# Half a weight chunk of step 28 loaded through GpSimd's queue, in seven DMAs of 17 partitions

## The reference

```
x = x + concat(retention, moba) @ w_out
h2 = rms_norm(x, norm2_w)
top_logit, top_e = top_k(h2 @ w_router + b_router, 4);  gate = softmax(top_logit)
for e in range(32):                     # for the tokens that picked e
    u = h2[tok] @ w1[e] + b1[e]         # 1024 x 2048: 8 MB of weights
    y = clamped_swiglu(u) @ w2[e] + b2[e]   # 1024 x 1024: 4 MB of weights
    x[tok] += gate * y
out = rms_norm(x, final_norm_w)
```

## Time and profile before

| | us |
|---|---|
| median of 3 runs | 1051.99 (1051.84 to 1052.05) |
| the profiled execution | 1051.63 |
| its span, first to last instruction | 1049.9 |
| outside the span | 1.7 |

### The profile page before, as it was taken

One profiled execution on the slowest core, in us unless ns is written; L12 is line 12 of the kernel. 1 busy time (PEld: TensorE's weight loads), 2 busy tenths in 40 slices (PEclk: granted clock), 3 DMA queues, 4 the chain that ended last, 5 costly groups with the idle time before them and its releaser, 6 DMA issues.

```text
span 1049.9 us, 11246 instructions
## 1 busy us (share of the span) xinstructions
PE 1029.5 (98%) x4918; PEld 415.3 (40%) x4918; DVE 221.3 (21%) x585; ACT 117.6 (11%) x223; POOL 0.2 (0%) x4
## 2 busy tenths in 40 slices
PE   9999999999999999999999999999999999999996
PEld 8888543333333333333333333333333333323332
DVE  2173442111111111111111111111111111111111
ACT  2131130000000000000000000000000000000002
POOL 0000000000000000000000000000000000000000
PEclk9999999999999999999999999999999999999999
DMA  9982999999999999999999999999999999999995
GB/s 320 369 365 81 354 364 400 410 428 424 429 428 431 433 432 428 431 429 430 432 423 431 429 435 428 434 424 433 428 428 427 430 432 431 432 429 424 428 422 214
DMA packets 39126, 424.62 MB, mean 404 GB/s; under 512 B 3512, under 2 KB 16320, under 8 KB 19744
## 3 DMA queue, kind: packets, MB, share of 16 engines
q1 hardware_dynamic: 38768, 423.51, 96.4%
q10 hardware_dynamic: 304, 0.33, 0.1%
HBM read 422.78 MB, written 1.05 MB: 404 GB/s over the span
## 4 chain that ended last, share of the span: by engine, by line
PE 89%; DMA 9%; DVE 1%; another core or an unknown queue 1%; issue 0%; ACT 0%; SPq 0%; DVEq 0%; ACTq 0%
PE PS L1444 39%; PE PS L1466 19%; DMA ring<-in_w 8%; PE PS L1122 8%; PE PS L1415 5%; PE PS L1398 4%; PE PS L1303 3%; PE PS L1259 3%; PE PS L1497 2%; PE PS L1407 2%; PE PS L1390 1%; DMA ring<-in_w_in 1%; PE PS L1571 0%; PE PS L1585 0%; PE PS L1192 0%
## 5 line engine op out<-in xcount | busy, mean ns | idle before, releaser
L1444 PE MATMUL PS<-ring,work 128*64 128x512 f32 x2040 | 450.2, 598 | 7.9 <-DMA ring<-in_w 6.8
L1444 PEld LDWEIGHTS PS<-ring,work 128*64 128x64 f32 x2040 | 143.7, 137 | 289.4 <-issue 275.8
L1466 PE MATMUL PS<-ring,work 128*64 128x512 f32 x1024 | 227.5, 596 | 0.7 <-DMA ring<-in_w 0.6
L1466 PEld LDWEIGHTS PS<-ring,work 128*64 128x64 f32 x1024 | 70.5, 137 | 154.7 <-issue 150.7
L1015 DVE TENSOR_SCALAR work<-PS 128x512 f32<-128x512 f32 x32 | 22.1, 691 | 398.3 <-PE PS L1444 398.3
L1122 PE MATMUL PS<-ring 128*128 128x256 f32 x384 | 85.4, 380 | 0.3 <-DMA ring<-in_w_in 0.3
L644 ACT ACTIVATE work<-work 128x512 f32<-128x512 f32 x32 | 20.2, 630 | 532.6 <-DVE work L1015 532.6
L1122 PEld LDWEIGHTS PS<-ring 128*128 128x128 f32 x384 | 72.0, 190 | 10.8 <-DMA ring<-in_w_in 0.7
L983 DVE TENSOR_TENSOR work<-PS,n2w 128x512 f32<-128x512 f32 x30 | 20.7, 692 | 228.4 <-PE PS L1407 228.4
L1415 PE MATMUL PS<-late,work 64*128 64x512 f32 x248 | 61.9, 616 | 0.0
L1398 PE MATMUL PS<-resid,work 128*64 128x512 f32 x248 | 58.5, 592 | 0.0
(11 more groups left out here) (173 smaller groups left out, 369.8 us busy)
## 6 DMA issues: line engine op xcount, KB each, us to landing
ring<-in_w SPq DMA_DIRECT2D x48, 4096.0 KB, 36.5
ring<-in_w SPq DMA_DIRECT2D x85, 2048.0 KB, 32.4
ring<-in_w SPq DMA_DIRECT2D x18, 1024.0 KB, 9.4
ring<-in_w_in SPq DMA_DIRECT2D x11, 1024.0 KB, 11.9
ring<-in_w_out SPq DMA_DIRECT2D x4, 1024.0 KB, 12.1
ring<-in_w SPq DMA_DIRECT2D x6, 512.0 KB, 6.1
ring<-in_w_in SPq DMA_DIRECT2D x2, 512.0 KB, 6.3
ring<-in_consts SPq DMA_DIRECT2D x1, 800.0 KB, 11.1
```

Source lines behind the costliest of these rows:

```text
L1444: last = mm(bank(v)[64 * half:64 * half + 64, :], gh[:, c, :], w[:, v * F + half * BANK:v * F + (half + 1) * BANK], start=False, stop=(c = ...
L1466: last = mm(out[64 * half:64 * half + 64, :], aT_n[:, c, 64 * h:64 * h + 64], ring[:, 2 * d + c // 2, cols:cols + BANK], start=(h == 0 and ...
```

## The change

One of the 2 MB loads, g = 170, is divided. Its second 1 MB (columns 2048 on of the pair's row, all 128 partitions) stays one DMA of SP with `pair_full`. Of its first 1 MB, SP loads only the last nine partitions. The other 119 are loaded by GpSimd, in seven DMAs of 17 partitions (8 KB each partition, 136 KB a DMA), issued after the same `chunk_used` count that SP waits for. After each of the seven, and twice more at the end, GpSimd issues a "tick", a DMA of 17 single float32 elements from `consts` into `n1w`, which nobody reads. That makes 16 DMAs of GpSimd. PE waits for the seven and for SP's nine rows before the first matmul on the pair.

```diff
+SPLIT, SPLIT_ROWS, SPLITS = (LAST - 3, W1_CHUNKS), 17, 7
...
+                elif isinstance(r, int) and (e, k) == SPLIT:
+                    src = w2_v[e - 1, down_chunk(j, k), :, :]
+                    rows = slice(SPLITS * SPLIT_ROWS, P)
+                    sp.dma_start(dst[rows, 0:2 * D], src[rows, 0:2 * D]).then_inc(rest_in, 16)
+                    sp.dma_start(dst[:, 2 * D:], src[:, 2 * D:]).then_inc(pair_full[d], 16)
...
+        @block.gpsimd
+        def _(pool):
+            e, k = SPLIT
+            d, g = pair_of(e, k), place_in_stream(e, k)
+            dst = ring[:, 2 * d:2 * d + 2, :].rearrange("p a n -> p (a n)")
+            src = w2_v[e - 1, down_chunk(e, k), :, :]
+            pool.wait_ge(wr_ready, 1)
+            pool.wait_ge(chunk_used, HEAD_CHUNKS + g - PAIRS + 1)
+
+            def tick(m):
+                at = 32 * (m // C)
+                pool.dma_start(n1w[at:at + SPLIT_ROWS, m % C:m % C + 1],
+                               consts[0:SPLIT_ROWS, m:m + 1]).then_inc(tick_in, 16)
+
+            for m in range(SPLITS):
+                rows = slice(m * SPLIT_ROWS, (m + 1) * SPLIT_ROWS)
+                pool.dma_start(dst[rows, 0:2 * D], src[rows, 0:2 * D]).then_inc(split_in, 16)
+                tick(m)
+            tick(SPLITS)
+            tick(SPLITS + 1)
+            pool.wait_ge(tick_in, 16 * (SPLITS + 2))
...
+                if isinstance(r, int) and (local_expert(i, j), k) == SPLIT:
+                    pe.wait_ge(split_in, 16 * SPLITS)
+                    pe.wait_ge(rest_in, 16)
```

More of the change, by code:

```diff
@@ L264, in layer_kernel @@
         pair_full = [sem(f"pair_full{d}") for d in range(PAIRS)]
+        split_in = sem("split_in")
+        tick_in = sem("tick_in")
+        rest_in = sem("rest_in")
         chunk_used = sem("chunk_used")
```

## The result

Measured side by side, the kernel before takes 1052.02 us (1051.84 to 1052.52, four runs) and the changed kernel 1062.26 us (1061.53 to 1064.44, four runs): a ratio of 1.0103, 95% interval 1.0091 to 1.0116. The change costs 10.2 us where 0.5 us of gain was forecast, and lies outside the range given. The profiled execution is the longest of the four, 1064.44 us, so its rows show some 2 us more than the median.

A forecast was written before the change was run, and what follows sets the result against it. The prediction took weight loads to pace the late kernel; +1.0 us at 929.28 and -1.5 us of later waits gave -0.5 us, from the median 1051.99 to 1051.5 us, range 1050.0 to 1060.0.

The forecast's parts named there:

- What bounds the kernel: Late part of the kernel: paced by weight loads at 427 GB/s; PE waits 7.4 us in all from 840 us on.
- The gain, at most 1.5 us: PE's waits after 929.28, of 0.49, 0.35 and 0.63 us, are all that faster transfers can give back.
- One 8 KB row costs its engine 0.307 us: Divided load: each row's engine time at 26.7 GB/s an engine, used to price every part of the change.
- Each lies on one engine: Each DMA of 17 partitions goes wholly to one engine, costing it 5.2 us instead of 2.46 us.
- the seven worse and nine better engines: Balance during the divided load: seven engines 2.8 us worse off, nine 2.15 to 2.46 us better off.
- What is overtaken, +1.0 us: GpSimd's rows delay the 4 MB load that step 28 awaits until 929.28: 0 to 1.9 us, taken as 1.0.
- Ticks, from nothing to 0.9 us: GpSimd's nine tiny DMAs of 17 elements: bounds of nothing and 0.9 us an engine.
- The added wait, taken as nothing: PE's matmuls at 940.84 also wait for GpSimd's rows, which have 57 us, against 15.7 to 26.1 us a large DMA.
- the rival: GpSimd's DMAs queue for each other, two large ones in flight: +6 to +47 us less 1.5, some 1070 us, chance 0.18.
- slower: Outcomes where the change costs time, by queueing GpSimd DMAs or by loading engines already behind: chance 0.18 + 0.16 = 0.34.
- The wrong engines: Large DMAs fall on engines already behind; landing at 929.28 comes 5.2 us later: +3.7 us, 1055.7 us, chance 0.16.
- No effect: Rows spread evenly or engines never the limit; 2.3 us later at 929, 1.5 back: +0.8 us, 1052.8, chance 0.15.

The follow-up runs named there:

- pool128: Kernel before, with the first 1 MB of g = 170 loaded by GpSimd as one DMA of all 128 partitions, no ticks: 1051.74 us.
- large7: Changed kernel without ticks; GpSimd still issues the seven loads of 17 partitions: 1065.16 us.
- ticks16: Kernel before, SP loading g = 170 whole, plus 16 ticks of 17 elements issued by GpSimd: 1051.74 us.
- pool128x4: Kernel before, with the first 1 MB loaded by GpSimd in four DMAs of 128 partitions, 2 KB each, no ticks: 1052.47 us.
- act128: Kernel before, with the first 1 MB loaded as one DMA of 128 partitions issued by ScalarE, no ticks: 1052.09 us.
- sp64_stride2: Kernel before, with the first 1 MB loaded by SP in two DMAs of 64 partitions, even ones then odd ones: 1051.83 us.
- sp32_stride4: Kernel before, with the first 1 MB loaded by SP in four DMAs of 32 partitions, four apart: 1051.51 us.
- pool32_stride4: Changed kernel, but GpSimd loads all 128 partitions in four DMAs of 32, four apart, each followed by three ticks: 1052.22 us.

## Why the prediction was wrong, step by step

**What bounds the kernel**: right, and it is why the miss is so large. The late kernel is paced by the loads, so nearly all of the 10.0 us of loading lost between 884 and 936 reaches the end.

**The gain, at most 1.5 us**: none of it came. The waits at 1017.88 and 1030.39 in the earlier trace rows stand unchanged in the rows after, 0.35 and 0.63 us, and the one of 0.49 us has become 1.23. The earlier trace rows was read as a reserve of balance that the relieved engines would give back. The drain after:

```profile
1042.00:1043.00 1.00, 0.84 (x4) 0.00 (x0) 0.00 (x0) 0.11 (x1) 0.00 (x0) 1.00 0.90 373
1044.00:1045.00 1.00, 1.00 (x8) 0.27 (x4) 0.00 (x0) 0.99 (x2) 0.00 (x0) 1.00 0.61 242
1046.00:1047.00 1.00, 1.00 (x8) 0.32 (x6) 0.00 (x0) 0.00 (x0) 0.00 (x0) 1.00 0.32 131
1048.00:1049.00 1.00, 1.00 (x6) 0.34 (x6) 0.00 (x0) 0.00 (x0) 0.00 (x0) 1.00 0.15 61
1050.00:1051.00 1.00, 1.00 (x8) 0.41 (x6) 0.00 (x0) 0.00 (x0) 0.00 (x0) 1.00 0.07 29
1051.00:1052.00 1.00, 1.00 (x8) 0.20 (x4) 0.00 (x0) 0.08 (x1) 0.00 (x0) 1.00 0.02 8
```

It takes some 12 us where it took 9, and its last six run at a share of 0.32 or less, so about five engines, and then fewer, were late together. The opposite of balance, and most of what the profiled span lost beyond the 10.0 us.

**"One 8 KB row costs its engine 0.307 us"**: this is the step that failed, and with it every term built on it. In pool128 GpSimd's 8 KB rows took 0.309 us in the median; in the changed kernel they took 0.41 us (0.43 in large7), and while they ran SP's 16 KB rows took 0.84 us instead of 0.61. The prediction counted bytes per engine and nothing else; it put at nothing what one load's rows do to another's, and that was nine tenths of the 10.6 us. It had the earlier trace rows only for loads of 128 partitions (eight rows for each engine, as it said), and carried their rate over to loads of 17, with no bound for the other case. It did say that it would be wrong "if a cost appears on the engines that these rows can't show". That was the case, and it deserved a place in the sum's bounds and a chance, since no row showed any load of fewer than 128 partitions beside a full queue.

**"Each lies on one engine"**: wrong. The queues of the changed kernel in 888 to 889.25 us (packets, MB, share of 16 engines):

```profile
q0 software_dynamic: 13, 0.07, 22.0%
```

0.07 MB are nine rows of 8 KB. In the packet records 17 such rows start between 888.21 and 891.64 us, up to four at once, and no other before 894.74. Seventeen is what the first large DMA has; it was issued at 884.44 and its first row moved 3.8 us later. The time to landing of the seven (issue to the last of 16 increments):

```profile
DMA to landing us min/median/max: 9.5/22.5/38.5
```

The first landed 9.5 us after its issue, 5.8 us after its first row. The prediction put 17 rows of one engine beside SP's queue at 15.7 us or more. The records do not name the engine, but linked as above GpSimd's packets in large7 (884 to 925 us) have between two 4-byte writes of an engine no row 47 times, one row twice and two rows nine times, never more. Nine engines, eight with two rows and one with one, make 17 and fit this. That the seven large DMAs lie on seven different engines, on which the seven worse and nine better engines and the 1.0 us at 929 stand, no run shows. By the prediction's own sums rows that are spread out give +0.8 us in place of -0.5, so this alone explains little of the miss.

**What is overtaken, +1.0 us**: there is such a term, but its place and price were off. The first wait that grows is the one before step 27's second half, 30 us ahead of 929.28: to 4.13 us in pool128, where the later waits then vanish, and to 5.61 in the changed kernel, where they do not. The wait before step 28's second half itself is 2.89 us where 2.26 stood; that half starts 14.1 us late because of what was lost ahead of it. pool128 overtakes with more bytes and ends with no loss, so the overtaking isn't the 10 us.

**Ticks, from nothing to 0.9 us**: they cost nothing that ticks16 shows (1051.74 against 1051.41 us). **The added wait, taken as nothing**: right, no wait stands before line 1498 at 953. The last of GpSimd's 8 KB rows ended at 927.07, 43 us after the first issue at 884.44, inside the 57 us that were there. **GpSimd's issues**: they took half a microsecond each and did not queue for each other. That only two of the large DMAs can be in flight was the rival's assumption, which no run shows: all seven were issued by 891.1, before the first landed at 893.9, so the rival fell. The issues:

```profile
884.44 0.65 POOL L568 DMA_DIRECT2D ring<-in_w  x1 [883.99 <-PE PS L1498]
885.08 0.52 POOL L563 DMA_DIRECT2D n1w<-in_consts  x1
...
891.05 1.08 POOL L563 DMA_DIRECT2D n1w<-in_consts  x2
```

**The rivals**: the sign of "slower" held 0.34 of the chance, and neither mechanism behind it was the one. "The wrong engines", with 1055.7 us, has the nearest figure, but its sign, a wait at 929 longer by 4 us or more, did not appear. The switch between queues, priced there at 0.3 us each, costs nothing that ticks16 or pool128x4 can show. "No effect" was right in one thing, that a second issuing engine by itself neither gained nor cost anything here: pool128, act128 and pool128x4 lie 0.0, 0.4 and 0.8 us over before, within their intervals.

## What to carry to other kernels

When loads pace a kernel, divide a load by columns and keep all 128 partitions in each part (pool128x4, by GpSimd), or take every second (sp64_stride2, by SP) or fourth partition (sp32_stride4 and pool32_stride4, by either). All were free here, while dividing 1 MB of 384 into blocks of neighbouring partitions cost 6.6 to 10.2 us, and 13.7 without the ticks. Every eighth partition cost 7.3. In a profile look at the DMA share and the GB/s together: here share 1.0 with fewer GB/s meant rows that took longer, and the bytes missing over the full rate were most of the time lost. And where the trace of before holds only one shape of load, its rate is no bound for another shape.

## What the runs showed of the hardware

- In the kernel before, from 884 to 950 us, each engine's share of a load of 128 partitions is eight rows and a write of 4 bytes (96 of 96 in the linked packet records). One load of 17 partitions gave an engine none, one or two rows (large7: 47, 2 and 9 times).
- Two queues with work waiting: an engine took one row of each in turn (pool128: 107 of 107), 8 KB rows of one and 16 or 32 KB rows of the other.
- A load of 64 neighbouring partitions and one of every second partition, same bytes, same queue: 243 and 426 GB/s over the same 16 us, at a DMA share of 0.99 and 1.00.
- The slowing reaches the rows of other loads: 16 KB rows of 128-partition loads took 0.84 us in the median beside the changed kernel's loads, 0.61 us before.
- Sixteen tiny DMAs of GpSimd beside a full queue: no cost (1051.74 against 1051.41 us). GpSimd issued the 16 in 8.19 us, one each 0.5 us.
- 1 MB by a second queue, beside and ahead of a queue 50 us long: no cost and no gain in the end, from GpSimd (1051.74) and from ScalarE (1052.09 us). The load that it overtakes first came 2.5 us later to PE, and later waits gave that back.
